# A mixer output product split into three passes, with its operands prepared during the convolution before it, and a reordered end

## The reference, cut to what matters

```python
a = rms_norm(h, norm_mix)
p = a @ w_in
y_hy = rms_norm(hyena_mixer(p[..., :D_HYENA_PROJ], ...), hyena_norm)   # two long convolutions
y_hg = hgrn2_mixer(p[..., D_HYENA_PROJ:], ...)                         # gated recurrence
h = h + jnp.concatenate([y_hy, y_hg], axis=-1) @ w_out                 # the mixer output product
h = h + hier_moe(rms_norm(h, norm_ffn), ...)                           # 64 experts, top 2 of each token
h = rms_norm(h, norm_final)
```

## Time and profile before

| | us |
|---|---|
| median of 3 runs | 3178.21 (3176.19 to 3183.2) |
| profiled execution, its own time | 3180.81 |
| its span, first to last instruction | 3179.0 |

### The profile page before, as it was taken

The page is one execution under the profiler, slowest core; times in us unless marked ns, Lnnn a source line. Parts: engine busy times, 40 slices in busy tenths (PEclk is TensorE's granted clock), DMA queues, the critical chain, the costliest instruction groups (busy, mean ns, idle before and its releaser), DMA issues.

```text
span 3179.0 us, 39693 instructions
## 1 busy us (share of the span) xinstructions
PE 2948.1 (93%) x15986; PEld 1975.8 (62%) x15986; DVE 1144.7 (36%) x1883; ACT 781.8 (25%) x1106; POOL 919.6 (29%) x755
## 2 busy tenths in 40 slices
PE   6999999999999999999999999999888888888887
PEld 4777778878788767888779895455333333333333
DVE  4566575561620163323333676614111111111112
ACT  2435542231322243323233541111000000000001
POOL 2333444455353304444433240001111111111111
PEclk9999999999999999999999999999999999999999
DMA  7324455542223302223312121048999999999997
GB/s 262 93 80 134 133 181 176 198 118 81 86 80 109 90 21 85 93 92 107 92 60 80 55 86 57 1 171 318 408 411 425 414 407 412 407 410 401 410 404 297
DMA packets 255936, 631.61 MB, mean 199 GB/s; under 512 B 19153, under 2 KB 208626, under 8 KB 230461
## 3 DMA queue, kind: packets, MB, share of 16 engines
q1 hardware_dynamic: 244989, 619.23, 52.1%
q0 software_dynamic: 10240, 8.43, 0.8%
q10 hardware_dynamic: 576, 2.10, 0.2%
HBM read 633.88 MB, written 20.97 MB: 206 GB/s over the span
## 4 chain that ended last, share of the span: by engine, by line
PE 60%; DMA 21%; DVE 7%; issue 5%; PEld 3%; ACT 2%; POOL 2%; SPq 0%; PEldq 0%; DVEq 0%; POOLq 0%; ACTq 0%
DMA arena<-in_w_up 20%; PE ps L545 12%; PE ps L547 12%; PE ps L546 12%; PE ps L4321 9%; PE ps L3480 2%; POOL ring_parts L427 2%; PE ps L2520 1%; PE ps L2519 1%; PE ps L2518 1%; PEld ps L545 1%; PEld ps L547 1%; PE ps L3695 1%; PE ps L2670 1%; PEld ps L546 1%
## 5 line engine op out<-in xcount | busy, mean ns | idle before, releaser
L427 POOL TENSOR_TENSOR ring_parts<-ring,arena_parts 128x512 fp32r<-128x512 f32 x544 | 721.5, 1360 | 1007.3 <-ACT arena_parts L401 773.3
L545 PE MATMUL ps<-arena_parts,arena_parts 128*128 128x512 f32 (+1 forms) x2012 | 749.6, 373 | 9.9 <-POOL ring_parts L427 4.6
L547 PE MATMUL ps<-arena_parts,ring_parts 128*128 128x512 f32 (+1 forms) x2012 | 741.2, 368 | 0.0
L4321 PE MATMUL ps<-arena 128*64 128x512 f32 x1008 | 494.2, 648 | 141.6 <-DMA arena<-in_w_up 93.2
L546 PE MATMUL ps<-hT_parts,arena_parts 128*128 128x512 f32 (+1 forms) x1648 | 596.0, 362 | 0.0
L4322 PE MATMUL ps<-arena 128*64 128x512 f32 x1008 | 495.5, 649 | 0.0
L545 PEld LDWEIGHTS ps<-arena_parts,arena_parts 128*128 128x128 f32 x2012 | 378.6, 188 | 86.9 <-issue 7.6
L4321 PEld LDWEIGHTS ps<-arena 128*64 128x64 f32 x1008 | 144.7, 149 | 458.1 <-issue 456.8
L547 PEld LDWEIGHTS ps<-arena_parts,ring_parts 128*128 128x128 f32 x2012 | 378.9, 188 | 69.1
L401 ACT ACTIVATE arena_parts<-ring 128x2048 fp32r<-128x2048 f32 (+1 forms) x103 | 206.9, 2013 | 635.8 <-PE ps L547 595.6
L546 PEld LDWEIGHTS ps<-hT_parts,arena_parts 128*128 128x128 f32 x1648 | 309.6, 188 | 49.9 <-issue 0.2
(11 more groups left out here) (644 smaller groups left out, 3597.6 us busy)
## 6 DMA issues: line engine op xcount, KB each, us to landing
arena<-in_w_down SPq DMA_DIRECT2D x63, 2048.0 KB, 23.0
arena<-in_w_gate SPq DMA_DIRECT2D x62, 2048.0 KB, 19.0
arena<-in_w_up SPq DMA_DIRECT2D x62, 2048.0 KB, 22.4
ring<-in_ffn_up SPq DMA_DIRECT2D x44, 1024.0 KB, 5.0
arena<-in_ada_w SPq DMA_DIRECT2D x14, 2048.0 KB, 9.9
ring<-in_ret_w_in SPq DMA_DIRECT2D x24, 1024.0 KB, 5.3
ring<-in_ffn_down SPq DMA_DIRECT2D x16, 1408.0 KB, 7.0
ring<-in_gdn_w_in SPq DMA_DIRECT2D x16, 1024.0 KB, 5.5
```

The costliest lines, as they stand in the source:

```text
L427: ins = pool.tensor_tensor(lower[:, at], whole[:, at], upper[:, at], ALU.subtract)
L545: pe.matmul(out, upper[:, r], self.upper[r][:, part], start=(r == 0), stop=False)
L547: ins = pe.matmul(out, lower[:, r], self.upper[r][:, part], start=False, stop=(r == self.tiles - 1))
L4321: pe.matmul(k.ps[upper, 2 + u, :], m.xeT[u][:, r, :], m.w_up[b][:, r, :], start=(r == 0), stop=(r == KD - 1))
```

## The change

1. `MixerOut`: the four recurrence row tiles are multiplied in the split form. The upper and lower parts of those four row tiles and of the weights' lower half are made ahead: ACT copies (`scalar_ahead`) behind its last work of the second convolution, POOL subtracts (`gpsimd_ahead`), in place. The upper parts take the buffers of the up weights of expert 1 and the down weights of expert 0.
2. `Experts.sync`: those two loads therefore wait for the last sum of the product (`mixed`).
3. `Experts.sync`: the last expert's down weights (`w_last`) are issued after the first halves of its gate and up weights have landed, and not after the second.
4. `Combine`: tile 3 is summed like the others.

```diff
+    SPLIT = KD - HYT
+    def scalar_ahead(self, act, stream):
+        act.wait_ge(self.k.sem("hy_filtered"), 14)
+        for r in range(self.SPLIT):
+            act.activation(self.x_upper[r], self.source(HYT + r), ACT.Copy).then_inc(self.sem("upper"), 1)
+        for c in range(KD // 2):
+            stream.landed(act, stream.n + c, 0)
+            act.activation(self.w_upper[c], self.split_weights(stream, c), ACT.Copy).then_inc(self.sem("upper"), 1)
+
+    def gpsimd_ahead(self, pool, stream):
+        for r in range(self.SPLIT):
+            self.wait(pool, "upper", r + 1)
+            whole = self.source(HYT + r)
+            pool.tensor_tensor(k.as_parts(whole), whole, self.x_upper[r], ALU.subtract).then_inc(self.sem("lower"), 1)
+        for c in range(KD // 2):
+            self.wait(pool, "upper", self.SPLIT + c + 1)
+            whole = self.split_weights(stream, c)
+            lower, step = k.as_parts(whole), self.SPLIT // 2
+            for at in (slice(0, step), slice(step, 2 * step)):
+                ins = pool.tensor_tensor(lower[:, at], whole[:, at], self.w_upper[c][:, at], ALU.subtract)
+            ins.then_inc(self.sem("lower"), 1)
...
-                ins = pe.matmul(self.bank(j), w[:, r, j % 2 * P:(j % 2 + 1) * P], self.source(r), start=(first and r == rows[0]), stop=(last and r == rows[-1]))
+                if r < HYT:
+                    ins = pe.matmul(self.bank(j), w[:, r, cols], self.source(r), start=begins, stop=ends)
+                    continue
+                self.wait(pe, "lower", self.SPLIT + j // 2 + 1)
...
+                pe.matmul(self.bank(j), w_upper, x_upper, start=begins, stop=False)
+                pe.matmul(self.bank(j), w_upper, x_lower, start=False, stop=False)
+                ins = pe.matmul(self.bank(j), w_lower[:, of, cols], x_upper, start=False, stop=ends)
...
         load_up(0, 0)
-        load_up(1, 1)
+        load_w(1, 1, "gate", "up", m.w_gate, "w_gate_2")
+        load_down(1, 1)
+        sp.wait_ge(k.sem("mixed"), 4 + KD)
+        load_w(1, 1, "up", "up", m.w_up, "w_up_2")
         load_down(0, 0)
-        load_down(1, 1)
         load_up_apart(self.THIRD)
...
-        sp.wait_ge(k.sem("apart_in"), 64)
+        for what in ("gate", "up"):
+            self.wait(sp, f"{what}_in0", 8 * NE)
         sp.dma_start(m.w_last, ...)
...
-        for u in range(LATE):
-            ins = self.spread(pe, TT - 1, u, first=(u == 0), last=(u == LATE - 1))
-        ins.then_inc(self.sem("combined"), 1)
+            self.spread(pe, TT - 1, u, first=(u == 0))
+        self.add(pe, TT - 1).then_inc(self.sem("combined"), 1)
...
-    def weigh(self, act):
-    def gpsimd(self, pool):
...
             self.sums(dve, st, 2)
             self.experts.lower_late(LATE - 1)
+            self.sums(dve, st, 3)
...
-                self.wait(dve, "combined", n + 1)
-                self.wait(dve, "weighed", 4)
-                dve.tensor_tensor(self.halves(self.sum[:, t]), self.halves(self.sum[:, t]), k.ps[:, self.BANKS[t]:self.BANKS[t] + 2, :], ALU.add).then_inc(self.sem("summed"), 1)
...
-            hyena.scalar(act); k.end(act, "scalar")
+            hyena.scalar(act)
+            mix_out.scalar_ahead(act, stream); k.end(act, "scalar")
...
-            hyena.gpsimd(pool); k.meet(pool, "gpsimd")
+            hyena.gpsimd(pool)
+            mix_out.gpsimd_ahead(pool, stream); k.meet(pool, "gpsimd")
```

More of the change, by code:

```diff
@@ L3452, in tensor, with __init__, split_weights @@
             ins.then_inc(self.sem("o"), 1)
-class MixerOut:
+class MixerOut(Signals):
     BANKS = (4, 5, 7, 0)
-    def __init__(self, k, stream, source, norm, after):
+    SPLIT = KD - HYT
+    def __init__(self, k, stream, source, norm, after, upper_room):
+        super().__init__(k, "mix", upper=self.SPLIT + KD // 2, lower=self.SPLIT + KD // 2)
         self.k, self.stream, self.source, self.norm, self.after = k, stream, source, norm, after
+        self.x_upper = [k.as_parts(upper_room.take(T)) for _ in range(self.SPLIT)]
+        self.w_upper = [k.as_parts(upper_room.take(self.SPLIT, 2 * P)) for _ in range(KD // 2)]
+    def split_weights(self, stream, c):
+        return stream.slot(stream.n + c, KD, 2 * P)[:, HYT:KD, :]
+    def scalar_ahead(self, act, stream):
[6 more added lines that the diff above has]
+    def gpsimd_ahead(self, pool, stream):
+        k = self.k
+        for r in range(self.SPLIT):
[9 more added lines that the diff above has]
+            ins.then_inc(self.sem("lower"), 1)
     def sync(self, sp):
@@ L3476, in terms @@
             w = stream.slot(n, KD, 2 * P)
+            cols = slice(j % 2 * P, (j % 2 + 1) * P)
+            w_lower = k.as_parts(self.split_weights(stream, j // 2))
             for r in rows:
@@ L3479, in terms @@
                     norm.wait(pe, "inverted", r + 1)
-                ins = pe.matmul(self.bank(j), w[:, r, j % 2 * P:(j % 2 + 1) * P], self.source(r), start=(first and r == rows[0]), stop=(last and r == rows[-1]))
+                begins, ends = first and r == rows[0], last and r == rows[-1]
+                if r < HYT:
+                    ins = pe.matmul(self.bank(j), w[:, r, cols], self.source(r), start=begins, stop=ends)
+                    continue
+                of = r - HYT
+                self.wait(pe, "lower", self.SPLIT + j // 2 + 1)
+                w_upper, x_upper, x_lower = self.w_upper[j // 2][:, of, cols], self.x_upper[of], k.as_parts(self.source(r))
+                pe.matmul(self.bank(j), w_upper, x_upper, start=begins, stop=False)
+                pe.matmul(self.bank(j), w_upper, x_lower, start=False, stop=False)
+                ins = pe.matmul(self.bank(j), w_lower[:, of, cols], x_upper, start=False, stop=ends)
             return ins
@@ L4626, in __init__ @@
     def __init__(self, k, m, experts):
-        super().__init__(k, "end", summed=TT, weighed=4, squared=TT, rooted=TT, inverted=TT, combined=TT, **{f"gathered{t}": 16 for t in range(TT)})
+        super().__init__(k, "end", summed=TT, squared=TT, rooted=TT, inverted=TT, combined=TT, **{f"gathered{t}": 16 for t in range(TT)})
         self.m, self.experts = m, experts
@@ L4642, in add @@
         for h, half in enumerate(HALF_D):
-            ins = pe.matmul(self.bank(t, h), self.k.ident[:], self.sum[:, t, half], start=(t == 0), stop=(t == 2))
+            ins = pe.matmul(self.bank(t, h), self.k.ident[:], self.sum[:, t, half], start=(t == 0), stop=(t >= 2))
         return ins
@@ L4699, in total_of @@
     def total_of(self, t):
-        return self.halves(self.sum[:, t]) if t == TT - 1 else self.k.ps[:, self.BANKS[t]:self.BANKS[t] + 2, :]
+        return self.k.ps[:, self.BANKS[t]:self.BANKS[t] + 2, :]
     def vector(self, dve, st, again=False):
@@ L4704, in vector @@
         if again:
-            for t in range(TT - 1):
+            for t in range(TT):
                 self.sums(dve, st, t)
@@ L4984, in _ @@
                 further.gpsimd(pool); k.meet(pool, "gpsimd", drain=False)
-                again.gpsimd(pool)
 def kernel(**inputs):
```

10 lines of the change are left out of this document (3 added, 7 removed).

## The result

| | before | after |
|---|---|---|
| median of the runs of this series | 3181.97 us (6 runs) | 3188.89 us (6 runs) |
| ratio | | 1.0022, 95% interval 1.0012 to 1.0032 |
| span of the profiled execution | 3179.0 us | 3186.9 us |
| mean granted clock of PE | 0.977 | 0.972 |

The change makes the kernel slower, by 7.0 us (3.8 to 10.2). I had forecast +4.4 us against 3178.21. The kernel before measured 3.8 us higher in this series than in the three runs shown, so of the 6.3 us between 3182.6 and 3188.9 some 3.8 are the level and 2.5 the terms; the forecast's sign was right, its size low, and the time lies above the range (3173 to 3187). It took both to get there: +7.0 us on the old level make 3185.2, and the forecast's +4.4 on the new one 3186.4.

A forecast was written before the change was run, and what follows sets the result against it. A chain of PE, DVE and ACT work bounds the kernel up to the first expert, the weight stream after it. Terms -5.6 + 7.7 + 1.7 + 1.8 - 1.2 = +4.4 us on 3178.21 gave 3182.6 us, range 3173 to 3187.

The forecast's parts named there:

- Edit 1: Mixer's output product on PE: 32 products in three split passes instead of f32, 5.6 us less.
- Edit 2: Second convolution: POOL's twelve subtractions hold up eight DVE operations with two SBUF inputs, +7.7 us (bounds 0 to 8.8).
- Rival A: Splits are free, POOL and DVE hardly meet: 3173.2 us, or 3171.4 without the DMA slip; chance 0.18.
- The clock behind it: PE's inverse transform idles twice; after the second gap 3.4 us at half speed lose 1.7 us (bounds 0 and 3.4).
- Edit 3: Two first weight loads come late: row writes use up 4 us slack, gather slips 0.5, shares DMA 1.3; +1.8 us (0 to 4).
- Edit 4: At the end, fourth token tile summed on DVE and PE: final square earlier, -1.2 us (bounds -2 and 0).
- Rival C: Weight stream absorbs a late first expert; only the end's -1.2 and part of the rest stay: 3177 to 3179; chance 0.12.
- Rival B: Inverse transform: POOL holds DVE up fully (8.5 us), PE's clock falls twice (3.4): +6.9, 3185.1 us; chance 0.20.

The follow-up runs named there:

- end_alone: Kernel before with only the end's two changes (tile 3 summed on DVE and PE, last down weights issued earlier): 3178.91 us, ratio 0.9990.
- end_pool: Kernel before with the end's two changes, plus one 128x512 GpSimd memset behind the third square: 3182.12 us, ratio 0.9992.

## Why the prediction was right in sign and wrong in size

**The level, 3.8 us.** I started from the median of three runs, 3178.21, and took the profiled execution to be 2.6 us slow. The six runs of this series have 3181.97, the later ones 3182.3 to 3183.9: it was the three that were low.

**Edit 1, -5.6 us: right.** The product is 64 f32 and 96 split records, and stretch b is 5.2 us shorter in every trace in which the clock does not fall in it; 4.8 timed, with the moved loads. The record of the first split matmul behind an f32 one is long, six times in the product, but it also starts early:
```profile
2115.12 3.68 PE L3514 MATMUL ps<-arena,ring 128*128 128x512 f32 x8
2118.24 0.79 PE L3519 MATMUL ps<-arena_parts,arena_parts 128*128 128x512 f32 x1
2118.87 0.39 PE L3520 MATMUL ps<-arena_parts,arena_parts 128*128 128x512 f32 x1
```
From 2115.12 to 2118.87 are 3.75 us, and 8 x 0.435 + 0.231 = 3.71. So a switch costs 0.04 us, six of them some 0.2 of the missing 0.4.

**Edit 2, +7.7 us: right.** 7.2 us in each of five traces with the late splits: 1.4 for the first pair, 3.8 for the four, 2.0 for the second pair, where I had 1.6, 4.1 and 2.0. The pair of the earlier trace rows was enough to price eight operations. The section of the Trainium skill that I cited ("SBUF — State Buffer", Who interferes with whom) agrees in which operations are held up: those with two inputs in SBUF, and no other. My bound from it for eight, 0 to 10 us, was too wide to decide. Rival A, free splits, falls.

**The clock behind it, +1.7 us: right in one execution, absent in another.** 0 in the first trace, 1.4 us in the second and in the kernel with the unread products, 0 in the two others with the late splits. The second gap was 2.6 us and not 4, because PE works on in between at half speed.

**Edit 3, +1.8 us: this is the step that failed.** Alone it costs 7.6 us. The text said that "the writes end 17.3 us after the last sum", as if loads and writes shared the engines without loss and the writes were done when the bytes were. They ended 19.6 us after it (2146.33 to 2165.90): the 6.3 MB took 17 us and not 15, and nearly 2 us more passed before SP's queue went on; what fills these is open. The 4 us of slack were used up and 3.6 more, where I had a slip of 0.5. The gate load then fell together with the gather. I had counted 1.3 us for that; PE's first use came 2.0 us later. And I had looked for gaps of PE only in the convolution. The late gather opens one of 5.6 us before expert 0; e is 2.3 us longer behind it, and in the second trace f 1.6 at expert 1. These falls of the clock are not shown to come from the gap, since kernels without it have some too. The 5.6 us of c and d do not hang on them, and already exceed my upper bound of 4, which was made of bytes alone.

**Edit 4, -1.2 us: right where I looked, short by what I did not look at.** The last square is 1.1 us earlier. The rest, 2.4 us in the trace (3.2 timed in all), is POOL's DRAIN. It is in no list of busy engines. It showed in the trace of before as 3.1 us of SP waiting at the last line, and in the 7.3 us between DVE's last operation and the end.

**Rival C falls.** Stretch g lies between 968.0 and 970.3 us in all executions, whether the first expert began early or late: the stream does not absorb, and a microsecond before the first expert is one at the end, within those 2.3 us.

**The sum.** The edits one by one come to +9.9 - 4.8 + 7.6 - 3.2 = +9.5 us, the changed kernel to +7.0 and +8.0, within the intervals. Two wrong terms, +5.8 and -2.0, partly hid each other, which was luck. Rival B's +6.9 us meets the measured +7.0 by luck as well: its 8.5 us for DVE and 3.4 for the clock were 7.2 and 0 to 1.4.

**What stays open.** In which executions the clock falls at experts 0 and 1. The kernels end_alone and end_pool have the same code there, yet d, e and f add up to 29.0 us in one and 34.3 in the other, 4.4 of the 5.3 in e and f; g gives 1.7 back. So a single trace can't tell whether the changed kernel suffers more of this than the kernel before.

## What to carry to other kernels

Splitting operands ahead of time on an idle POOL cost DVE nothing where DVE read PSUM or rested, and 7.2 us where it had two inputs in SBUF; look for DVE's rests before choosing the place (here 15.9 us lay just ahead). A buffer borrowed from a prefetch costs what the prefetch collides with when it comes late, small writes and gathers above all: borrow halves, and give them back one by one. An engine may have a long DRAIN behind its last work: compare the last output write with the end of the span. And start from more than three runs where the change is 0.2%.

## What the runs showed that I had not expected

- The last DRAIN of GpSimd takes 10.6 to 11.7 us, even where its last work is a memset of 0.53 us; where POOL works near the end it ends 10.6 to 11.9 us after that work. The memset cost 4.4 and 9.2 us at the end of the span, the second 9.6 us timed.
- Four 512 KB row writes that took 2.6 us (median) took 9.8 us behind two 2 MB loads of another queue, 3.9 us behind two of 1 MB.
- PE's granted clock fell to 0.50 behind a gap of 1.56 us in one kernel and not behind one of 2.56 us in another; with the same code it fell in one execution and not in the next, and stretches e and f moved by 4.4 us.
